# Three output projections go from plain float32 products to products of split operands in three passes, with their weights split in halves on ScalarE and GpSimd

## The chip, the core and the metric

The kernel runs on one core of a Trainium2 chip. The time is that of the device for one launch, in microseconds (us). Five engines work side by side, each with its own queue of instructions in program order: PE is TensorE (matrix products), DVE is VectorE, ACT is ScalarE, POOL is GpSimd, and SP issues the transfers. They wait for one another only by semaphores that the program names. On TensorE the profile shows weight loads (PEld) apart from the products (PE).

## The reference

Four layers of a transformer on 512 tokens of width 1024; the first two also carry 256 context tokens. All of it is float32. Each layer is an attention of some kind, an output projection and a residual sum; the last two layers have a gated feed-forward block behind that. The three output projections that the change touches are these products of a 512x1024 activation with a 1024x1024 weight:

```
y = jnp.dot(o.reshape(h.shape[0], h.shape[1], C_WIDTH) * jax.nn.silu(z_x), w_out)   # odd_mixer, od_w_out: "od_out"
...
x = x + gate * y
```

The third and fourth layer multiply their attention's result by even_w_out_2 ("e2_out") and odd_w_out_2 ("df_out") in the same way and add it to x without a gate.

## The kernel before, in words

Activations lie with features on the 128 partitions and tokens along the free dimension: X is 8 chunks of 128 features x 512 tokens. Weights come from HBM as a stream of tiles of 128x1024 float32 (512 KB), one for each 128 columns of output, into a ring of 8 slots (WT). SP refills a slot when the semaphore tile_used says that PE is through with the tile before it; w_ready{slot} tells that a tile has landed. STREAM sets the order of the tiles: od_out (8 tiles), e2_in (24), e2_out (8), up0 (44), down0 (22), df_in (24), df_out (8), up1 (44), down1 (22).

There are two ways to multiply. The three output projections use the plain one, project_pe (L277): for each of 8 tiles 8 products of 128x128 by 128x512 in float32, 64 in all, straight from the tile in WT and the attention's output (QO or OFE). Most other products use split operands: an activation or a weight x is written as hi, which is x rounded to the format fp32r (written by ACT), and lo = x - hi (written by DVE or POOL), and the product is hi*hi + hi*lo + lo*hi, three passes in fp32r. For that each weight tile has to be split before PE can use it.

- e2_in, df_in (class Projected, PE at L767 to L769), up0 and up1 (split_w_act, PE at L607 to L609) split whole tiles: ACT writes hi (1024 columns), DVE writes lo, into W_SPLIT with two places. Their first two tiles have a place of their own, W_EARLY, so that the first four tiles are split while the projection before still runs; PE takes tiles 0 and 1 interleaved (first_two_pe, L580 to L582), as chunks of the input become ready.
- ev_in, ev_out and the odd layer's input split in halves of 512 columns: ACT writes hi of a half (L513, L1360, L1369), POOL writes lo (L532, L1522, L1531), into W_HALF, which holds one half for h=0 and one for h=1. ACT may write half h of the next tile only when PE has used that half (half_used, tile_used). This is a ring: PE frees a half, ACT, then POOL refill it while PE works on the other.

Around an output projection the order is this. The attention's last unit ends with a DVE instruction (finish, L1781, or L1920 in the fourth layer) that raises at_out; PE waits for it (att.wait) and starts. For each finished tile t DVE adds it to X (residual_one, L652 with a gate, L650 without), ACT writes H_HI, chunk t of the next block's input times its gain (late_hi_act, L358), and DVE writes H_LO (residual_split_dve, L401). Before, DVE and ACT come to this only after they have split the next block's weight tiles 0 to 3, which arrive one by one as PE frees slots. Behind the last tile ACT squares X (L367) and DVE sums the squares (L377) for the norm.

Of the kernel before, what the change touches and what calls it, by code (L numbers as in the profile page):

```python
# [77 lines left out]
def program(nc, tokens, cond, weights, vec, con, gate_w, rpb, late, lam_in, out):  # L78
    ctx = ExitStack()
    with ctx:  # L80
# [79 lines left out]
        W_EARLY = over("W_EARLY", "SB", BIG + 4096, [128, 2, 2, TILE])  # L160

        def split_of(t):

            return W_EARLY[:, t] if t < 2 else W_SPLIT[:, t % 2]

# [185 lines left out]

        def late_hi_act(act, name):

            h0 = split_at[name][0]
            prev = LATE_NORMS[name][1]
            for c in range(KC):
                act.wait_ge(sem("evac_dve"), evacuated(prev)[1] + c + 1)
                act.activation(H_HI[:, c, :], X[:, c, 0:L], ACT.Identity, bias=NIL, scale=gain_late(name, c)).then_inc(sem("h_hi"), 1)  # L358
# [51 lines left out]
        def split_w_act(act, name, take, before=None):  # L410
# [3 lines left out]
            def body(q, s, rnd, slot):  # L414
                t = 8 * q + s if isinstance(q, int) else None
                if t == 0:
                    before(act)
                if t == 4:
                    late_hi_act(act, name)
                    late_squares_act(act, name)  # L420
                act.wait_ge(sem(f"w_ready{slot}"), (rnd + 1) * 16)
                if t is None or t >= 4:

                    act.wait_ge(sem("tile_used"), q * 8 + (g0 + s - 1))
                dst = W_SPLIT[:, s % 2] if t is None else split_of(t)
                act.activation(dst[:, 0, :], W[:, slot, :], ACT.Copy).then_inc(sem("w_hi"), 1)  # L426
# [34 lines left out]
        def low_w_dve(v, name, t, slot):  # L461

            w0 = split_at[name][1]
            v.wait_ge(sem("w_hi"), w0 + t + 1)
            v.tensor_tensor(split_of(t)[:, 1, :], W[:, slot, :], split_of(t)[:, 0, :].bitcast(F32), ALU.subtract)\
             .then_inc(sem("w_low"), 1)


        half_at = {"ev_in": 0, "ev_out": EV_CHUNKS, "od_q": EV_CHUNKS + 8}
# [96 lines left out]
        def first_two_pe(pe, name, banks_free):  # L566
# [3 lines left out]
            for k in range(KC + 1):  # L570
                for t in range(2):
# [7 lines left out]
                    hi, lo = (W_EARLY[:, t, x, c * 128:c * 128 + 128] for x in range(2))  # L579
# [142 lines left out]
        class Projected:  # L722
# [77 lines left out]
            def act(self, act, before=None):  # L800
                if before:
                    before(act)
                for t in range(26):
                    if t == (3 if self.early else 4):
# [3 lines left out]
                    if t < 24:  # L808
# [5 lines left out]
                        act.activation(split_of(t)[:, 0, :], W[:, (self.g0 + t) % SLOTS, :], ACT.Copy).then_inc(sem("w_hi"), 1)  # L814
# [7 lines left out]
                    if t < 4:  # L822
                        continue
                    if t == 4:
# [18 lines left out]
            def low(self, v, t):  # L843
                v.wait_ge(sem("w_hi"), self.w0 + t + 1)
                v.tensor_tensor(split_of(t)[:, 1, :], W[:, (self.g0 + t) % SLOTS, :], split_of(t)[:, 0, :].bitcast(F32), ALU.subtract)\  # L845
# [14 lines left out]
            def dve(self, v, add):  # L860
                for t in range(3 if self.early else 4):
                    self.low(v, t)
                residual_split_dve(v, self.name, add)
                if self.early:
                    self.low(v, 3)
# [20 lines left out]
            def values(self, eng):  # L886

                eng.wait_ge(sem("v_out"), self.value0 + 8)

# [283 lines left out]
        class Window:  # L1173
# [75 lines left out]
            def out_pe(self, pe):  # L1249
                for t in range(8):  # L1250
                    if t >= 4:
                        pe.wait_ge(sem("evac_dve"), self.d_ev + t - 3)
                    for h in range(2):
                        pe.wait_ge(sem("half_lo"), 2 * (self.gate0 + t) + h + 1)
                        for c in range(4 * h, 4 * h + 4):
                            if t == 0:
                                pe.wait_ge(sem("od_lo"), c + 1)
# [20 lines left out]
            def first_pe(self, pe):  # L1278
                pe.wait_ge(sem("first_lo"), 4)
                pe.wait_ge(sem("rs_log"), self.i + 1)  # L1280
                for c in range(KC):
                    pe.wait_ge(sem("od_lo"), KC + c + 1)
# [94 lines left out]
            def out_act(self, act):  # L1377
                for k, c in enumerate(self.order):
                    if c < 4:
                        act.wait_ge(sem("at_out"), att_mla.b["out"] + 2 * c + 2)  # L1380
                    act.activation(self.O_HI[:, k, :], PROJ[:, ZA + c, :], ACT.Copy).then_inc(sem("od_hi"), 1)
                for t in range(1, 8):
# [3 lines left out]
                    if t in (3, 4):  # L1386
                        act.wait_ge(sem(f"raw_in{t - 3}"), 32)
                        act.activation(self.FIRST[:, t - 3, 0, :], self.RAW[:, t - 3, :], ACT.Copy).then_inc(sem("od_hi"), 1)
# [7 lines left out]
                for c in range(KC):  # L1396
                    act.wait_ge(sem("od_normed"), KC + c + 1)
                    act.activation(HN_HI[:, c, 0:L], H[:, c, 0:L], ACT.Identity, bias=MOD[:, 24 + c, 0:1]).then_inc(sem("od_hi"), 1)
# [1407 lines left out]
```

## Time and profile before

| what | value |
|---|---|
| median of 3 runs | 2560.61 us (2560.12 to 2560.93) |
| the profiled execution: its time / its span | 2561.2 us / 2559.4 us |
| PE busy / DVE / ACT / POOL | 95% / 45% / 38% / 12% |
| mean granted TensorE clock | 0.983 |

The span runs from the first to the last instruction; 1.8 us of the execution's time lie outside it. All times in rows are us from the span's start. L numbers are lines of the kernel before. A row of the timeline gives start, duration, engine, line, operation, what it writes and reads and how many instructions are merged into it (xN); in square brackets the idle time before it and who ended it. Matrix products overlap: a product has a record of some 0.39 us, but the next one starts 0.23 us later, so the cost of one is the distance of starts. A plain float32 product shows as two records. In the clock's column 1.00 is the level of 2.4 GHz and 0.50 that of 1.2 GHz.

### The profile page before, as it was taken

The page shows a single profiled execution, that of the slowest core. Times are in us where ns is not written, and L with a number is a line of the kernel's source. Part 1 is how long each engine was busy: PE and PEld are TensorE (multiplying, and loading weights), DVE is VectorE, ACT ScalarE, POOL GpSimd, SP SyncE. Part 2 cuts the span into 40 slices and gives each one's busy share as a digit, 9 for nine tenths or more (in the row PEclk, how much of TensorE's full clock was granted, in tenths as well). Part 3 has the DMA queues.
Part 4 walks back from the last instruction along what each step waited for, and adds up shares of the span by engine and source line. Part 5 has one row for each costly group of instructions (what it writes and reads, how often), then busy time and mean ns, then how long its engine had stood idle before and what let it go on. Part 6 is the DMA issues. An engine that isn't in the chain of part 4 may idle for free.

```text
span 2559.4 us, 32847 instructions
## 1 busy us (share of the span) xinstructions
PE 2440.0 (95%) x12608; PEld 1799.0 (70%) x12608; DVE 1140.5 (45%) x1867; ACT 969.6 (38%) x1596; POOL 306.4 (12%) x206
## 2 busy tenths in 40 slices
PE   7999899889999999999999999999999889999998
PEld 4888665356878876664776568888877654888886
DVE  4000542544442204553345347666454462666744
ACT  4111434444344424552325343333252461433323
POOL 2233001100223330000000000003400000000142
PEclk9999799999999999999999999999999999999999
DMA  7112241010132222102220022323222101323231
GB/s 298 58 58 66 75 149 49 9 50 1 42 109 65 68 73 75 51 18 97 91 82 26 26 91 91 98 90 99 92 90 83 50 1 58 99 91 98 91 99 41
DMA packets 51872, 191.67 MB, mean 75 GB/s; under 512 B 5755, under 2 KB 6139, under 8 KB 51484
## 3 DMA queue, kind: packets, MB, share of 16 engines
q1 hardware_dynamic: 51740, 189.83, 22.5%
q8 instruction: 93, 1.52, 0.2%
q14 instruction: 39, 0.32, 0.0%
HBM read 187.71 MB, written 2.10 MB: 74 GB/s over the span
## 4 chain that ended last, share of the span: by engine, by line
PE 88%; ACT 4%; DVE 4%; issue 2%; DMA 0%; POOL 0%; SPq 0%; ACTq 0%; DVEq 0%; POOLq 0%
PE PS L277 7%; PE PS L609 6%; PE PS L607 6%; PE PS L608 6%; PE PS L1631 5%; PE PS L1658 4%; PE PS L2239 3%; PE PS L2241 3%; PE PS L2240 3%; PE PS L1644 3%; PE PS L1338 3%; PE PS L561 3%; PE PS L562 3%; PE PS L560 3%; PE PS L938 2%; PE PS L769 2%
## 5 line engine op out<-in xcount | busy, mean ns | idle before, releaser
L457 POOL TENSOR_TENSOR W_SPLIT<-WT,W_SPLIT 128x1024 fp32r<-128x1024 f32 x44 | 106.6, 2424 | 1455.4 <-ACT W_SPLIT L449 1331.9
L607 PE MATMUL PS<-H_HI,W_SPLIT 128*128 128x512 f32 x672 | 265.5, 395 | 0.0
L609 PE MATMUL PS<-H_HI,W_SPLIT 128*128 128x512 f32 x672 | 264.9, 394 | 0.0
L608 PE MATMUL PS<-H_LO,W_SPLIT 128*128 128x512 f32 x672 | 264.6, 394 | 0.0
L426 ACT ACTIVATE W_SPLIT<-WT 128x1024 fp32r<-128x1024 f32 x84 | 89.0, 1060 | 290.5 <-PE PS L609 267.3
L277 PE MATMUL PS<-SB,WT 128*128 128x512 f32 x384 | 167.3, 598 | 5.2 <-DVE SB L1781 3.1
L2570 DVE TENSOR_TENSOR W_SPLIT<-WT,W_SPLIT 128x1024 fp32r<-128x1024 f32 x80 | 98.0, 1225 | 151.8 <-ACT W_SPLIT L426 151.7
L2555 DVE TENSOR_TENSOR G_LO<-SB,G_HI 128x512 fp32r<-128x512 f32 x44 | 102.6, 2331 | 115.0 <-ACT G_HI L2395 115.0
L608 PEld LDWEIGHTS PS<-H_LO,W_SPLIT 128*128 128x128 f32 x672 | 126.0, 188 | 30.3 <-issue 0.5
L607 PEld LDWEIGHTS PS<-H_HI,W_SPLIT 128*128 128x128 f32 x672 | 126.2, 188 | 30.0 <-issue 0.5
L609 PEld LDWEIGHTS PS<-H_HI,W_SPLIT 128*128 128x128 f32 x672 | 126.2, 188 | 29.7
L277 PEld LDWEIGHTS PS<-SB,WT 128*128 128x128 f32 x384 | 73.3, 192 | 97.4 <-issue 91.5
L1644 PEld LDWEIGHTS PS<-SB 128*128 128x128 f32 x768 | 84.4, 142 | 79.6 <-issue 68.8
L2239 PE MATMUL PS<-G_HI,W_SPLIT 128*128 128x512 f32 x352 | 138.8, 394 | 0.2
L2241 PE MATMUL PS<-G_HI,W_SPLIT 128*128 128x512 f32 x352 | 138.0, 392 | 0.0
L2240 PE MATMUL PS<-G_LO,W_SPLIT 128*128 128x512 f32 x352 | 136.6, 388 | 0.0
L1644 PE MATMUL PS<-SB 128*128 128x128 f32 x768 | 112.9, 281 | 21.8 <-ACT SB L1705 19.2
L562 PE MATMUL PS<-HN_HI,W_HALF 128*128 128x512 f32 x368 | 124.1, 337 | 0.0
L561 PE MATMUL PS<-HN_LO,W_HALF 128*128 128x512 f32 x368 | 124.1, 337 | 0.0
L560 PE MATMUL PS<-HN_HI,W_HALF 128*128 128x512 f32 x368 | 123.7, 336 | 0.0
L845 DVE TENSOR_TENSOR W_SPLIT<-WT,W_SPLIT 128x1024 fp32r<-128x1024 f32 x44 | 53.9, 1226 | 154.6 <-ACT W_SPLIT L814 154.6
L1705 ACT ACTIVATE SB<-PS 128x512 f32<-128x512 f32 x120 | 64.8, 581 | 144.4 <-PE PS L1644 144.4
(322 smaller groups left out, 5158.5 us busy)
## 6 DMA issues: line engine op xcount, KB each, us to landing
WT<-weights SPq DMA_DIRECT2D x316, 512.0 KB, 3.5
SB<-weights SPq DMA_DIRECT2D x13, 512.0 KB, 12.7
SB<-rpb SPq DMA_DIRECT2D x8, 512.0 KB, 5.1
HT<-rpb SPq DMA_DIRECT2D x8, 512.0 KB, 4.4
XT<-tokens SPq DMA_DIRECT2D x4, 768.0 KB, 6.9
out<-HT SPq DMA_DIRECT2D x4, 512.0 KB, 2.6
SB<-late SPq DMA_DIRECT2D x1, 1280.0 KB, 5.7
SB<-con SPq DMA_DIRECT2D x1, 1248.0 KB
```

What stands on the lines that cost most here:

```text
L277: last = pe.matmul(PS[0:m, bank, 0:hi - lo], W[:, slot, c * 128:c * 128 + m], src[:, c, lo:hi], start=(c == 0), stop=(c == k - 1))
L560: pe.matmul(dst, hi, HN_HI[:, c, at:end], start=(c == 0), stop=False)
L561: pe.matmul(dst, hi, HN_LO[:, c, at:end], start=False, stop=False)
L562: last = pe.matmul(dst, lo, HN_HI[:, c, at:end], start=False, stop=(c == KC - 1))
L607: pe.matmul(PS[:, s, :], hi, H_HI[:, c, :], start=(c == 0), stop=False)
L608: pe.matmul(PS[:, s, :], hi, H_LO[:, c, :], start=False, stop=False)
L609: last = pe.matmul(PS[:, s, :], lo, H_HI[:, c, :], start=False, stop=(c == KC - 1))
L1631: last = pe.matmul(PS[:, self.bank(s, a) + b // 512, 0:e - b], self.q_of(pair, a)[:, 128 * t:128 * t + 128], self.k_of(pair, a)[:, lo + b: ...
L1644: last = pe.transpose(PS[:, 4 + k % 2, (b - b0) * 128:(b - b0) * 128 + 128], self.p(s, b // nb)[:, (b % nb) * 128:(b % nb) * 128 + 128], I ...
L2239: pe.matmul(PS[:, n, :], hi, G_HI[:, s % 2, :], start=first, stop=False)
L2240: pe.matmul(PS[:, n, :], hi, G_LO[:, s % 2, :], start=False, stop=False)
L2241: last = pe.matmul(PS[:, n, :], lo, G_HI[:, s % 2, :], start=False, stop=end)
```

## The change

The three projections get a class Output. PE multiplies with split operands, three passes per chunk. The attention's output O is split chunk by chunk: ACT writes O_HI (L934 of the changed kernel), DVE writes O_LO over O itself (L949). The weight tiles are split in halves of 512 columns, hi on ACT (L929) and lo on POOL (L965), into a new OUT_HALF with one place for each half; the first tile's halves are split ahead (before the attention od, and at tile 22 of e2_in and df_in). The work for the next block is woven in tile by tile: at tile t ACT writes the halves of tile t+1, then H_HI of chunk t, then hi of one whole tile of the next block (t = 1 to 4); DVE adds tile t, writes H_LO of chunk t-1 and lo of one whole tile (four times). up0 and up1 get an early place at another address, W_EARLY_UP.

```diff
+        class Output:
+            def pe(self, pe):
+                pe.wait_ge(sem("evac_dve"), ev_base[self.name][1])
+                for t in range(8):
+                    for h in range(2):
+                        pe.wait_ge(sem("half_lo"), 2 * (self.half0 + t) + h + 1)
+                        for c in range(4 * h, 4 * h + 4):
+                            if t == 0:
+                                pe.wait_ge(sem("o_lo"), self.lo0 + c + 1)
+                            hi, lo = (OUT_HALF[:, h, k, (c % 4) * 128:(c % 4) * 128 + 128] for k in range(2))
+                            pe.matmul(PS[:, t, :], hi, self.O_HI[:, c, :], start=(c == 0), stop=False)
+                            pe.matmul(PS[:, t, :], hi, self.O_LO[:, c, :], start=False, stop=False)
+                            last = pe.matmul(PS[:, t, :], lo, self.O_HI[:, c, :], start=False, stop=(c == KC - 1))
+                        last.then_inc(sem("tile_used" if h else "half_used"), 1)
+            def hi(self, act, t, h):
+                g = self.g0 + t
+                act.wait_ge(sem(f"w_ready{g % SLOTS}"), (g // SLOTS + 1) * 16)
+                if t and h == 0:
+                    act.wait_ge(sem("half_used"), self.used0 + t)
+                elif t:
+                    act.wait_ge(sem("tile_used"), g)
+                act.activation(OUT_HALF[:, h, 0, :], W[:, g % SLOTS, h * 512:h * 512 + 512], ACT.Copy).then_inc(sem("half_hi"), 1)
+            def act(self, act):
+                for c in range(KC):
+                    act.wait_ge(sem("at_out"), self.att.b["out"] + c + 1)
+                    act.activation(self.O_HI[:, c, :], self.O[:, c, :], ACT.Copy).then_inc(sem("o_hi"), 1)
+                f0 = FIRST_TILE[self.following]
+                for t in range(8):
+                    if t < 7:
+                        self.hi(act, t + 1, 0)
+                        self.hi(act, t + 1, 1)
+                    late_hi_one(act, self.following, t)
+                    if 1 <= t < 5:
+                        k = t - 1
+                        act.wait_ge(sem(f"w_ready{(f0 + k) % SLOTS}"), ((f0 + k) // SLOTS + 1) * 16)
+                        act.activation(split_of(self.following, k)[:, 0, :], W[:, (f0 + k) % SLOTS, :], ACT.Copy).then_inc(sem("w_hi"), 1)
+            def dve(self, v, add):
+                for c in range(KC):
+                    v.wait_ge(sem("o_hi"), self.hi0 + c + 1)
+                    v.tensor_tensor(self.O_LO[:, c, :], self.O[:, c, :], self.O_HI[:, c, :].bitcast(F32), ALU.subtract).then_inc(sem("o_lo"), 1)
+                h0 = split_at[self.following][0]
+                for c in range(KC + 1):
+                    if c < KC:
+                        add(c)
+                    if c >= 1:
+                        v.wait_ge(sem("h_hi"), h0 + c)
+                        v.scalar_tensor_tensor(H_LO[:, c - 1, :], X[:, c - 1, 0:L], gain_late(self.following, c - 1),
+                                               H_HI[:, c - 1, :].bitcast(F32), ALU.mult, ALU.subtract).then_inc(sem("h_lo"), 1)
+                    if 2 <= c < 6:
+                        low_w_dve(v, self.following, c - 2, (FIRST_TILE[self.following] + c - 2) % SLOTS)
+            def pool(self, g):
+                for t in range(8):
+                    for h in range(2):
+                        g.wait_ge(sem("half_hi"), 2 * (self.half0 + t) + h + 1)
+                        g.tensor_tensor(OUT_HALF[:, h, 1, :], W[:, (self.g0 + t) % SLOTS, h * 512:h * 512 + 512],
+                                        OUT_HALF[:, h, 0, :].bitcast(F32), ALU.subtract).then_inc(sem("half_lo"), 1)
...
-            project_pe(pe, "od_out", 8, QO, KC, L)
+            out_od.pe(pe)
...
-            project_pe(pe, "e2_out", 8, OFE, KC, L)
+            out_e2.pe(pe)
...
-            project_pe(pe, "df_out", 8, OFE, KC, L)
+            out_df.pe(pe)
```

What this does to DVE's queue at the first of the three projections (od_out), from the attention's last instruction on. In the kernel before (L1781 ends the attention, L845 are the next block's weight tiles, L652 the residual sums, L401 H_LO):

```order
L1781 TENSOR_TENSOR SB<-PS,SB 128x512
L845 TENSOR_TENSOR W_EARLY<-WT,W_EARLY 128x1024 x2
L845 TENSOR_TENSOR W_SPLIT<-WT,W_SPLIT 128x1024 x2
L652 SCALAR_TENSOR_TENSOR XT<-PS,SB,XT 128x512 x2
L401 SCALAR_TENSOR_TENSOR H_LO<-XT,SB,H_HI 128x512
```

In the changed kernel, at the same place of DVE's queue (L949 is O_LO, L655 the residual sums, L956 H_LO, L466 the next block's weight tiles):

```order
L1859 TENSOR_TENSOR SB<-PS,SB 128x512
L949 TENSOR_TENSOR O_LO_65<-SB,O_HI_64 128x512 x8
L655 SCALAR_TENSOR_TENSOR XT<-PS,SB,XT 128x512 x2
L956 SCALAR_TENSOR_TENSOR H_LO<-XT,SB,H_HI 128x512
L655 SCALAR_TENSOR_TENSOR XT<-PS,SB,XT 128x512
L956 SCALAR_TENSOR_TENSOR H_LO<-XT,SB,H_HI 128x512
L466 TENSOR_TENSOR W_EARLY<-WT,W_EARLY 128x1024
L655 SCALAR_TENSOR_TENSOR XT<-PS,SB,XT 128x512
L956 SCALAR_TENSOR_TENSOR H_LO<-XT,SB,H_HI 128x512
L466 TENSOR_TENSOR W_EARLY<-WT,W_EARLY 128x1024
```

So eight O_LO now stand between the attention's end and the residual sums, and each of the four weight tiles stands right behind an H_LO.

ACT's queue at the same place, before (L1705 belongs to the attention; L814 the weight tiles, L358 H_HI, L367 the squares):

```order
L1705 ACTIVATE SB<-PS 128x512 x2
L814 ACTIVATE W_EARLY<-WT 128x1024 x2
L814 ACTIVATE W_SPLIT<-WT 128x1024 x2
L358 ACTIVATE H_HI<-XT,SB 128x512 x8
L367 ACTIVATE XT<-XT 128x2x256 x8
```

and in the changed kernel (L934 O_HI, L929 hi of the halves of od_out's tiles, L359 H_HI, L944 the next block's tiles):

```order
L1783 ACTIVATE SB<-PS 128x512 x2
L934 ACTIVATE O_HI_64<-SB 128x512 x8
L929 ACTIVATE OUT_HALF<-WT 128x512 x2
L359 ACTIVATE H_HI<-XT,SB 128x512
L929 ACTIVATE OUT_HALF<-WT 128x512 x2
L359 ACTIVATE H_HI<-XT,SB 128x512
L944 ACTIVATE W_EARLY<-WT 128x1024
L929 ACTIVATE OUT_HALF<-WT 128x512 x2
L359 ACTIVATE H_HI<-XT,SB 128x512
L944 ACTIVATE W_EARLY<-WT 128x1024
```

Between two pairs of halves, on which PE now waits, ACT has an H_HI that waits for DVE's residual sum and, four times, a whole tile of the next block. POOL, which had nothing in these stretches, gets 16 lo halves in each.

## Rows read from the trace of the kernel before

**Rows 1.** The page: the chain that ended last, shares of the span by engine.
```profile
PE 88%; ACT 4%; DVE 4%; issue 2%; DMA 0%; POOL 0%; SPq 0%; ACTq 0%; DVEq 0%; POOLq 0%
```

**Rows 2.** Timeline of PE: the three output projections, and what follows the first.
```profile
1151.60 55.20 PE L277 MATMUL PS<-SB,WT 128*128 128x512 f32 x128 [1.52 <-DVE SB L1781]
1206.23 0.79 PE L580 MATMUL PS<-H_HI,W_EARLY 128*128 128x512 f32 x1
...
1442.88 55.20 PE L277 MATMUL PS<-SB,WT 128*128 128x512 f32 x128 [1.56 <-DVE SB L1781]
...
2117.52 56.90 PE L277 MATMUL PS<-SB,WT 128*128 128x512 f32 x128 [2.13 <-DVE SB L1920]
```

**Rows 3.** Timeline of PE: first product of e2_in's tile 2 and of tile 3.
```profile
1217.77 0.40 PE L767 MATMUL PS<-H_HI,W_SPLIT 128*128 128x512 f32 x1
...
1223.34 0.39 PE L767 MATMUL PS<-H_HI,W_SPLIT 128*128 128x512 f32 x1
```

**Rows 4.** Timelines of DVE and PE: two attentions' ends, and ev_out's start.
```profile
1150.85 0.69 DVE L1781 TENSOR_TENSOR SB<-PS,SB 128x512 f32<-128x512 f32 x1
...
651.69 0.42 DVE L1781 TENSOR_TENSOR SB<-PS,SB 128x256 f32<-128x256 f32 x1
...
653.25 0.47 PE L1261 MATMUL PS<-O_HI,W_HALF 128*128 128x512 f32 x1 [2.07 <-DVE O_LO L1462]
```

**Rows 5.** Windows behind three starts of PE (ev_out, df_out, od_out); the clock stands behind POOL.
```profile
654.20:657.60 3.40, 3.40 (x12) 2.92 (x12) 3.40 (x5) 1.02 (x2) 0.00 (x0) 0.50 0.00 0
2118.50:2122.00 3.50, 3.50 (x6) 1.44 (x5) 0.00 (x0) 0.00 (x0) 0.00 (x0) 0.51 0.00 0
1151.60:1155.00 3.40, 3.40 (x8) 1.62 (x9) 0.00 (x0) 0.00 (x0) 0.00 (x0) 1.00 0.73 211
```

**Rows 6.** Timelines of ACT, POOL and PE: the ring of halves, odd layer's input.
```profile
888.20 0.63 ACT L1369 ACTIVATE W_HALF<-WT 128x512 fp32r<-128x512 f32 x1 [2.15 <-PE PS L1310]
...
886.13 1.30 POOL L1531 TENSOR_TENSOR W_HALF<-WT,W_HALF 128x512 fp32r<-128x512 f32 x1 [1.48 <-ACT W_HALF L1369]
888.91 2.01 POOL L1531 TENSOR_TENSOR W_HALF<-WT,W_HALF 128x512 fp32r<-128x512 f32 x1 [1.48 <-ACT W_HALF L1369]
...
890.50 0.39 PE L1310 MATMUL PS<-HN_HI,W_HALF 128*128 128x512 f32 x1
...
891.32 0.39 PE L1309 MATMUL PS<-HN_LO,W_HALF 128*128 128x512 f32 x1
```

**Rows 7.** Timelines of DVE and POOL where both read two tensors from SBUF.
```profile
738.47 0.74 DVE L1482 SCALAR_TENSOR_TENSOR HN_LO<-HT,SB,HN_HI 128x512 fp32r<-128x512 f32 x1
739.13 0.68 DVE L1479 TENSOR_TENSOR HT<-HT,SB 128x512 f32<-128x512 f32 x1
...
738.65 2.34 POOL L1531 TENSOR_TENSOR W_HALF<-WT,W_HALF 128x512 fp32r<-128x512 f32 x1 [22.09 <-ACT W_HALF L1369]
...
876.33 2.98 DVE L1513 SCALAR_TENSOR_TENSOR SB<-SB 128x768 f32<-128x768 f32 x2
...
876.48 2.01 POOL L1531 TENSOR_TENSOR W_HALF<-WT,W_HALF 128x512 fp32r<-128x512 f32 x1 [1.48 <-ACT W_HALF L1369]
```

**Rows 8.** Timelines of ACT and DVE beside od_out: weight tiles, H_HI, residual sums.
```profile
1162.58 1.06 ACT L814 ACTIVATE W_EARLY<-WT 128x1024 fp32r<-128x1024 f32 x1 [16.43 <-DMA WT<-weights]
...
1188.30 0.82 ACT L358 ACTIVATE H_HI<-XT,SB 128x512 fp32r<-128x512 f32 x1 [0.78 <-DVE XT L652]
...
1163.74 1.23 DVE L845 TENSOR_TENSOR W_EARLY<-WT,W_EARLY 128x1024 fp32r<-128x1024 f32 x1 [12.19 <-ACT W_EARLY L814]
...
1199.97 0.75 DVE L652 SCALAR_TENSOR_TENSOR XT<-PS,SB,XT 128x512 f32<-128x512 f32 x1 [5.46 <-PE PS L277]
```

**Rows 9.** Timeline of ACT: idle time where first halves go; df attention's end.
```profile
982.39 1.28 ACT L1696 ACT_TABLE_LOAD   x1 [4.15 <-DVE SB L1747]
...
1345.68 1.06 ACT L814 ACTIVATE W_SPLIT<-WT 128x1024 fp32r<-128x1024 f32 x1 [4.49 <-PE PS L787]
...
2116.05 0.63 ACT L1888 ACTIVATE SB<-SB 128x512 f32<-128x512 f32 x1
```

More of the change, by code:

```diff
@@ L408, in behind, with split_w_act @@
             return (q if s >= k else q - 1), (s - k) % 8
-        def split_w_act(act, name, take, before=None):
+        def split_w_act(act, name, take):
             g0, (h0, w0, n) = FIRST_TILE[name], split_at[name]
@@ L415, in body @@
                 t = 8 * q + s if isinstance(q, int) else None
-                if t == 0:
-                    before(act)
+                if t is not None and t < 4:
+                    return
                 if t == 4:
-                    late_hi_act(act, name)
                     late_squares_act(act, name)
                 act.wait_ge(sem(f"w_ready{slot}"), (rnd + 1) * 16)
[L422 to L426, printed above, removed]
+                act.wait_ge(sem("tile_used"), q * 8 + (g0 + s - 1))
+                act.activation(W_SPLIT[:, s % 2, 0, :], W[:, slot, :], ACT.Copy).then_inc(sem("w_hi"), 1)
                 if t == 4:
@@ L464, in low_w_dve @@
             v.wait_ge(sem("w_hi"), w0 + t + 1)
-            v.tensor_tensor(split_of(t)[:, 1, :], W[:, slot, :], split_of(t)[:, 0, :].bitcast(F32), ALU.subtract)\
+            v.tensor_tensor(split_of(name, t)[:, 1, :], W[:, slot, :], split_of(name, t)[:, 0, :].bitcast(F32), ALU.subtract)\
              .then_inc(sem("w_low"), 1)
-        half_at = {"ev_in": 0, "ev_out": EV_CHUNKS, "od_q": EV_CHUNKS + 8}
+        half_at = {"ev_in": 0, "ev_out": EV_CHUNKS, "od_q": EV_CHUNKS + 8,
+                   "od_out": (EV_CHUNKS + 38, EV_CHUNKS + 40), "e2_out": (EV_CHUNKS + 46, EV_CHUNKS + 48),
+                   "df_out": (EV_CHUNKS + 54, EV_CHUNKS + 56)}
         def first_hi(act, t, h):
@@ L578, in first_two_pe @@
                         pe.wait_ge(sem("h_lo"), h0 + c + 1)
-                    hi, lo = (W_EARLY[:, t, x, c * 128:c * 128 + 128] for x in range(2))
+                    hi, lo = (early_of(name)[:, t, x, c * 128:c * 128 + 128] for x in range(2))
                     pe.matmul(PS[:, t, :], hi, H_HI[:, c, :], start=(c == 0), stop=False)
@@ L798, in pe, with act @@
                         pe.matmul(PS[:, 6 + r % 2, :], std[0], QKE[:, r, :], start=True, stop=True).then_inc(sem("qk_turned"), 1)
[L800 to L804, printed above, removed]
+            def act(self, act, output):
+                for t in range(0 if self.early else 4, 26):
+                    if t == 3:
                         late_hi_act(act, self.name)
@@ L823, in act @@
                         continue
+                    if t == 22:
+                        output.hi(act, 0, 0)
+                        output.hi(act, 0, 1)
                     if t == 4:
@@ L858, in turned, with dve @@
                 v.tensor_tensor(x, self.T1[:, r % 2, :], self.T2[:, r % 2, :], ALU.add).then_inc(sem("qk_done"), 1)
[L860 to L863, printed above, removed]
+            def dve(self, v, add=None):
                 if self.early:
+                    for t in range(3):
+                        self.low(v, t)
+                    residual_split_dve(v, self.name, add)
                     self.low(v, 3)
@@ L1380, in out_act @@
                         act.wait_ge(sem("at_out"), att_mla.b["out"] + 2 * c + 2)
-                    act.activation(self.O_HI[:, k, :], PROJ[:, ZA + c, :], ACT.Copy).then_inc(sem("od_hi"), 1)
+                    act.activation(self.O_HI[:, k, :], PROJ[:, ZA + c, :], ACT.Copy).then_inc(sem("o_hi"), 1)
                 for t in range(1, 8):
@@ L1985, in program @@
                              mask=causal_mask(lambda u: 0), values_in=qkv_df.values, sm_at=PE_AT + 5120, rt_at=PE_AT + 6144, sq_at=PE_AT + 6656, wide=512)
+        OUT_HALF = over("OUT_HALF", "HT", KC * L, [128, 2, 2, TILE // 2])
+        out_od = Output(0, "od_out", "e2_in", att_od, 8192)
+        out_e2 = Output(1, "e2_out", "up0", att_e, 4096)
+        out_df = Output(2, "df_out", "up1", att_df, 4096)
         G = view(BIG, FC, L)
@@ L2602, in down_one @@
                 return add
-            def low_first(name):
-                for t in range(4):
-                    low_w_dve(v, name, t, (FIRST_TILE[name] + t) % SLOTS)
-            qkv_e2.dve(v, residual_one(v, "od_out", L, lambda t, b: MOD[:, 40 + t, 0:1]))
+            out_od.dve(v, residual_one(v, "od_out", L, lambda t, b: MOD[:, 40 + t, 0:1]))
+            qkv_e2.dve(v)
             qkv_e2.heads(v)
```

66 lines of the change are left out of this document (42 added, 24 removed).

## The prediction

> **What bounds the kernel now.** I read the chain that ended last first: 88% of it is PE [rows 1], and DMA has no share, so time is won where PE does less or waits less. Then PE's timeline at the three output projections [rows 2]. Each runs without a gap from its first product to its last. The reader is to see two things: 64 float32 products take 1206.23 - 1151.60 = 54.63 us from the first to the next block's first product, 0.854 us each; and PE starts right behind the attention's last DVE instruction (1150.85 + 0.69 = 1151.54 [rows 4], PE at 1151.60), after a pause of 1.52, 1.56 and 2.13 us. The record of each projection is 0.57 us longer than that distance (1151.60 + 55.20 against 1206.23), so e2_out takes 54.63 and df_out 56.90 - 0.57 = 56.33 us. The three make **165.6 us**, all on the path. Beside them DVE and ACT are idle most of the time and POOL altogether.
>
> **The change part by part.**
>
> *The products.* The passes in fp32r are in the trace: e2_in's tile 2 begins at 1217.77, tile 3 at 1223.34 [rows 3], so 24 passes take 5.57 us, 0.232 each. Three passes per chunk are 0.696 us where the float32 product took 0.854. A projection of 192 passes takes 8 x 5.57 = 44.56 us.
>
> *The switch of format.* The first fp32r product behind float32 ones has a record of 0.79 us instead of 0.39 [rows 2, 3]. This switch now lies at the projection's beginning, where PE's start is counted anew below (and that row includes it). At the end it goes: -0.40 us.
>
> *The start.* PE may start when O_LO of chunk 0 is there, and DVE writes it only behind the attention's last instruction. ev_out already starts so: DVE ends at 651.69 + 0.42 = 652.11 and PE begins at 653.25, 1.14 us later [rows 4]. The pieces there are 768 wide. By the records of 512 and 1024 columns, 0.68 and 1.23 us [rows 7, 8], 256 columns less are 0.27 us less, so 0.87 us against 0.06 before: **+0.81 us**. The other seven chunks follow at some 0.6 us each and PE needs one each 0.70 us, so they hide behind its passes. ACT's O_HI is earlier still: in the last attention ACT is free at 2116.05 + 0.63 = 2116.68 [rows 9], and DVE's last instruction there ends some 0.8 us behind that, as PE's start at 2117.52 shows.
>
> *The clock.* A pause costs more than itself. Behind the pause of 2.07 us ahead of ev_out and that of 2.13 us ahead of df_out the granted clock falls to the 1.2 GHz level for 3.4 us; behind the pause of 1.52 us it stays at 2.4 GHz [rows 2, 4, 5]. At half the clock 3.4 us of work are 1.7 us of delay, and df_out's 56.33 - 54.63 = 1.70 us show just that. With 0.81 us more the pauses become 2.33, 2.37 and 2.94 us, all on the longer side. I therefore charge **1.7 us** to each projection (df_out has it already). Bounds: 0 and 1.7.
>
> *The ring of halves.* This is the part that could go wrong: POOL is much slower than DVE at it, and the two halves give each refill only the 12 passes, 2.79 us, of the other half. The odd layer's input runs the same ring at that very pitch: POOL starts at 886.13 and 888.91, 2.78 us apart [rows 6]. ACT takes the half 0.71 us ahead of POOL, POOL needs 1.30 us, and PE does not wait. When POOL took 2.01 us, 0.71 more, PE's two steps from 890.50 to 891.32 took 0.82 us instead of 0.46: a wait of 0.36. So the ring has **0.35 us to spare** per half.
>
> *POOL against DVE.* Why 2.01 us? In the like case DVE's instruction with two inputs from SBUF begins at 876.33, POOL's split at 876.48 has to wait, and then the second such DVE instruction waits for POOL (the two last 2.98 us together, where one of 512 columns takes 0.74) [rows 7]. The one shuts the other out. The last 0.12 us of a DVE record don't count: POOL's record of 2.34 us from 738.65 has its own 1.30 us from 739.69, and DVE's ran to 739.13 + 0.68 = 739.81. Now lay out a tile from its first pass. The tile before ends at +0.16; ACT starts hi of half 1 at +0.25, POOL wants to start at +0.96. DVE starts the residual sum at about +0.2, and 0.66 us later (the distance 738.47 to 739.13 [rows 7]) H_LO, from +0.86. It lets go of SBUF 0.62 us on, at +1.48. POOL is 0.52 us late, and 0.17 of it is more than the ring spares. This happens in the six tiles in which an H_LO follows a residual sum: **+1.0 us** per projection. Then DVE's weight tile waits until POOL ends at +2.8 and holds SBUF until +3.9; POOL's next split is wanted at 2.79 + 0.96 = +3.75: 0.15 late, which is spared. Bounds for the whole item: 0, and the second rival below.
>
> *ACT's queue.* Behind hi of half 1 ACT waits for the residual sum (done at about +0.98), writes H_HI (0.82) and the weight tile (1.06) [rows 8] and is free at +2.86; the next half is wanted at 2.79 + 0.25 = +3.04. It fits, with 0.18 us left. The tile of the next block lands 4.1 us behind the end of the projection's tile whose slot it takes (1162.58 against 1151.60 + 6.83 [rows 2, 8]); ACT asks for it one tile and 1.8 us later, 7.4 us. Nothing waits.
>
> *What moves at no cost.* The first tile's halves take ACT 2 x 0.63 us [rows 6] inside idle stretches of 4.15 and, ahead of tile 23 of e2_in, 4.49 us [rows 9]; POOL is idle there. Without that cover it would be 1.3 us each. The next block's four whole-tile splits and H_HI, H_LO were beside PE's work before and still are.
>
> **The sum.** Per projection 44.56 + 0.81 + 1.7 + 1.0 - 0.40 = 47.67 us, three of them 143.0 us against 165.6: a gain of 22.6 us. The profiled execution took 2561.2 us, 0.6 us over the median. 2561.2 - 22.6 = 2538.6, in terms of the median **2538.0 us**.
>
> **A rule on the shared pair.** The Trainium skill (SBUF — State Buffer, "SBUF: two separate sides") says that a VectorE instruction with two SBUF inputs and a GpSimd instruction exclude each other by a lock held for the whole instruction, not by sharing bandwidth. The rows of 2.01 us agree. Taken to the letter, with H_LO's whole record of 0.74 us instead of 0.62, POOL would be 0.12 us later in 18 tiles, 2.2 us in all: 2540.2 us. I take the 0.62, as worked out from 738.65 above.
>
> **The rivals.**
> 1. *Forecast: POOL gets its turn behind H_LO.* 2538.0 us. Without the drop of the clock at od_out and e2_out 2534.6, at none of the three 2532.9; with the whole-record lock 2540.2. For it: both DVE instructions of L1513 stood back to back, and POOL still went between them [rows 7]. Chance 0.68, own range 2531 to 2542.
> 2. *DVE keeps the lock through H_LO and the weight tile behind it.* At 738.47 and 739.13 DVE's two instructions went first and POOL's record grew to 2.34 us [rows 7]. Against it: that second instruction had no semaphore to wait for in the program, while L1513's and all of the new ones have one. If it holds, POOL is held until 1.48 + 0.05 + 1.11 = +2.64, 1.68 us late, a PE wait of 1.33 instead of 0.17, in four tiles of each projection: 12 x 1.16 = 13.9 us more, **2551.9 us**. Chance 0.20.
> 3. *Both, and more delays in the ring.* If every one of the 42 refills lost half a microsecond beyond what the ring spares, 21 us would go and 2559 us be left, no change that can be told. Rows of 1.30 us speak against it wherever DVE is quiet, and DVE has only some 2.5 us of work in each 5.57. Chance 0.08 for this and all between 2552 and 2566.
> 4. *Slower: the next block's weight tile in ACT's queue.* It stands between two refills, so a late transfer stops PE through ACT and POOL, where before it stopped nothing. It has 7.4 - 4.1 = 3.3 us in hand, and 0.5 more from ACT and the ring. To pay back 22.6 us with 12 such waits takes 1.9 us each, a landing 9.8 us behind the slot's release; from 2.3 us each on the kernel is slower by over 0.2%, about **2566 us**. All transfers seen here land in half that. Chance 0.04.
>
> **How the numbers follow.** A measurement of this kernel can tell about 0.2%, 5.1 us, from no change. Faster by more than that is all below 2555.5 us: 0.68 + 0.20 and a part of the third, 0.91. Within 0.2%: 0.05. Slower: 0.04. The range reaches over the forecast's own bounds and the second rival, **2531 to 2553 us**.
>
> **What would show it.** In the changed profile PE's starts of tiles should lie 5.57 to 5.75 us apart and the first pass 0.87 us behind the attention's last DVE instruction; POOL's 48 splits should last 1.30 us, or 1.8 in six per projection, and 2.9 to 3.0 us in four if the second rival holds. The clock should be 0.50 in a stretch of 3.4 us behind each start. From there to the next block's first product 47.7 us, or 52.3 with the second rival. The forecast is wrong if ACT's waits for a transfer end behind PE's need, if POOL's record in the new ring is above 2 us in most tiles, or if PE gains a pause ahead of the next block's first tile, where H_LO of the last chunks comes as late after the last product as before.

## The result

| | before | after |
|---|---|---|
| median | 2560.36 us (2555.07 to 2560.93, 4 runs) | 2528.39 us (2527.76 to 2538.56, 4 runs) |
| the profiled execution: time / span | 2561.2 / 2559.4 us | 2528.24 / 2526.5 us |

The ratio is 0.9889, with a 95% interval of 0.9861 to 0.9917: faster. It is the ratio of the means, 2559.2 and 2530.8 us, which lie 28.4 us apart; the medians lie 32.0 us apart, as one of four runs in each row stands far from the rest. The forecast was 2538.0 us, a ratio of 0.9912. That is inside the interval, but the median lies 2.6 us below the range of 2531 to 2553. A repeat (below) gave 2530.97 us and 0.9892.

The page of the changed kernel: span, busy time of each engine, and the chain that ended last (compare [rows 1]).

```profile
span 2526.5 us, 33417 instructions
PE 2404.6 (95%) x12800; PEld 1828.9 (72%) x12800; DVE 1166.3 (46%) x1891; ACT 1011.4 (40%) x1668; POOL 376.9 (15%) x254
...
PE 88%; ACT 5%; DVE 5%; issue 2%; DMA 1%; SPq 0%; POOL 0%; DVEq 0%; ACTq 0%; POOLq 0%
```

POOL has 70 us more work and is still not on the chain. PE has 35 us less.

Windows of the changed kernel: the three projections from the first product to the next block's first, then the four stretches around them. The columns are window, its length, PE, PEld, DVE, ACT, POOL busy with their instructions, granted clock, share of DMA, GB/s.

```profile
1145.61:1192.74 47.13, 47.13 (x193) 36.80 (x193) 22.22 (x24) 18.26 (x25) 20.81 (x14) 0.96 0.37 120
1428.22:1473.46 45.24, 45.23 (x192) 35.71 (x193) 21.82 (x24) 20.95 (x30) 20.84 (x14) 1.00 0.25 82
2093.26:2141.29 48.03, 48.03 (x192) 37.78 (x193) 21.80 (x24) 20.88 (x30) 20.73 (x14) 0.94 0.24 77
0.00:1145.61 1145.61, 1067.75 (x6616) 784.40 (x6617) 404.73 (x753) 460.15 (x764) 201.50 (x164) 0.98 0.21 73
1192.74:1428.22 235.48, 226.78 (x1355) 166.20 (x1354) 116.13 (x258) 98.40 (x219) 3.07 (x2) 1.00 0.17 57
1473.46:2093.26 619.80, 595.76 (x2654) 467.46 (x2652) 353.77 (x569) 255.22 (x428) 56.52 (x24) 0.99 0.24 78
2141.29:2526.50 385.21, 373.96 (x1603) 300.59 (x1601) 225.85 (x242) 137.50 (x174) 53.45 (x22) 0.99 0.26 86
```

By [rows 2] the three stretches took 54.63, 54.63 and 56.33 us before. They now take 140.4 us instead of 165.6, 25.2 less. The other 7.7 us of the span's difference of 32.9 lie outside, most of it ahead of od_out: 1145.61 against 1151.60, though the pause ahead of PE's start has grown by 0.8 us. Little in that stretch was changed, and the experiments ask first what this is.

The timeline of PE in the changed kernel: the first product of each of od_out's tiles, and of e2_in.

```profile
1145.61 0.47 PE L917 MATMUL PS<-O_HI,OUT_HALF 128*128 128x512 f32 x1 [2.33 <-DVE O_LO L949]
...
1152.84 0.39 PE L917 MATMUL PS<-O_HI,OUT_HALF 128*128 128x512 f32 x1
...
1158.44 0.39 PE L917 MATMUL PS<-O_HI,OUT_HALF 128*128 128x512 f32 x1
...
1164.16 0.39 PE L917 MATMUL PS<-O_HI,OUT_HALF 128*128 128x512 f32 x1
...
1169.88 0.39 PE L917 MATMUL PS<-O_HI,OUT_HALF 128*128 128x512 f32 x1
...
1192.74 0.39 PE L583 MATMUL PS<-H_HI,W_EARLY 128*128 128x512 f32 x1
```

The first tile takes 7.23 us (a drop of the clock), the second 5.60, the third and later ones 5.72. The first product of e2_in now has a record of 0.39 us and the next starts 0.23 later. Before, the record was 0.79 [rows 2].

The drops behind the starts of od_out and df_out, and the starts of two passes inside the second:

```profile
1147.10:1150.50 3.40, 3.40 (x10) 2.64 (x9) 2.58 (x5) 0.56 (x1) 0.00 (x0) 0.50 0.96 391
2093.30:2099.40 6.10, 6.10 (x15) 4.75 (x16) 4.02 (x7) 3.04 (x6) 0.00 (x0) 0.50 0.00 0
...
2094.25 0.63 PE L919 MATMUL PS<-O_HI,OUT_HALF 128*128 128x512 f32 x1
2094.68 0.63 PE L917 MATMUL PS<-O_HI,OUT_HALF 128*128 128x512 f32 x1
```

At 1.2 GHz a pass starts 0.43 us behind the one before, at 2.4 GHz 0.23 us. So a pass loses some 0.45 of its time at the low clock, not half: a drop of 3.4 us costs 1.55 us here, where it cost the plain float32 products 1.70 us (56.33 against 54.63).

DVE, POOL and ACT of the changed kernel in the fourth tile, which begins at 1164.16.

```profile
1164.36 0.75 DVE L655 SCALAR_TENSOR_TENSOR XT<-PS,SB,XT 128x512 f32<-128x512 f32 x1 [4.31 <-PE PS L919]
1165.02 0.74 DVE L956 SCALAR_TENSOR_TENSOR H_LO<-XT,SB,H_HI 128x512 fp32r<-128x512 f32 x1
1165.68 2.31 DVE L466 TENSOR_TENSOR W_EARLY<-WT,W_EARLY 128x1024 fp32r<-128x1024 f32 x1
...
1162.21 1.29 POOL L965 TENSOR_TENSOR OUT_HALF<-WT,OUT_HALF 128x512 fp32r<-128x512 f32 x1 [1.01 <-ACT OUT_HALF L929]
1165.12 1.79 POOL L965 TENSOR_TENSOR OUT_HALF<-WT,OUT_HALF 128x512 fp32r<-128x512 f32 x1 [1.63 <-ACT OUT_HALF L929]
1167.93 1.30 POOL L965 TENSOR_TENSOR OUT_HALF<-WT,OUT_HALF 128x512 fp32r<-128x512 f32 x1 [1.01 <-ACT OUT_HALF L929]
...
1165.86 1.04 ACT L944 ACTIVATE W_EARLY<-WT 128x1024 fp32r<-128x1024 f32 x1
1167.22 0.63 ACT L929 ACTIVATE OUT_HALF<-WT 128x512 fp32r<-128x512 f32 x1 [0.31 <-PE PS L919]
```

POOL's record starts 0.10 us after H_LO's and lasts 1.79 us instead of 1.29, and then DVE's weight tile lasts 2.31 us instead of 1.23: POOL had its turn between DVE's two instructions. The next split is undisturbed, at 1.30. ACT has 0.31 us in hand before its next half.

### The profile page after: what moved, and what is told of

Read it like the earlier page. It is cut to its first block, busy times and chain, and to the rows that moved or that the text cites. A ratio compares the mean times of both kernels' runs of the same rounds, so it can differ in the third digit from the quotient of the medians.

```text
span 2526.5 us, 33417 instructions
## 1 busy us (share of the span) xinstructions
PE 2404.6 (95%) x12800; PEld 1828.9 (72%) x12800; DVE 1166.3 (46%) x1891; ACT 1011.4 (40%) x1668; POOL 376.9 (15%) x254
## 3 DMA queue, kind: packets, MB, share of 16 engines
q8 instruction: 95, 1.56, 0.3%
## 4 chain that ended last, share of the span: by engine, by line
PE 88%; ACT 5%; DVE 5%; issue 2%; DMA 1%; SPq 0%; POOL 0%; DVEq 0%; ACTq 0%; POOLq 0%
PE PS L612 6%; PE PS L610 6%; PE PS L611 6%; PE PS L1709 5%; PE PS L1736 4%; PE PS L2328 3%; PE PS L2326 3%; PE PS L2327 3%; PE PS L1722 3%; PE PS L1416 3%; PE PS L564 3%; PE PS L565 3%; PE PS L563 3%; PE PS L1016 2%; PE PS L772 2%; PE PS L770 2%
## 5 line engine op out<-in xcount | busy, mean ns | idle before, releaser
L427 ACT ACTIVATE W_SPLIT<-WT 128x1024 fp32r<-128x1024 f32 x80 | 84.8, 1060 | 267.3 <-PE PS L612 267.3
L965 POOL TENSOR_TENSOR OUT_HALF<-WT,OUT_HALF 128x512 fp32r<-128x512 f32 x48 | 71.0, 1482 | 737.6 <-ACT OUT_HALF L929 737.6
L815 ACT ACTIVATE W_SPLIT<-WT 128x1024 fp32r<-128x1024 f32 x42 | 44.5, 1059 | 172.7 <-PE PS L772 114.6
```

## Experiments

**What is the gain outside the projections?** The kernel before and the changed kernel, each once more without an edit.

> The kernel before, unchanged, with a profile of its own, to see what the two first profiles differ by ahead of the change's place. In them the first float32 product of od_out starts at 1151.60 us before and the first split one at 1145.61 us after, and the time at the 1.2 GHz level up to there is 54.6 against 37.5 us. If this is the clock's own variation (A), this run's od_out starts anywhere between about 1145 and 1155 us, about half a microsecond earlier for each microsecond less at the low level, and the three stretches keep 54.63 us, or 56.3 with a drop of the clock in them. If it comes from something the change does (B), od_out starts at 1151.6 within 0.5 us again, with 54 to 55 us at the low level.

Measured: 2559.08 us (2555.47 to 2561.71, 10 runs), ratio 1.0001 (0.9991 to 1.0011). Windows of its profiled execution, up to od_out and od_out:

```profile
0.00:1148.52 1148.52, 1070.84 (x6616) 784.88 (x6616) 404.62 (x751) 454.86 (x754) 200.35 (x162) 0.98 0.21 73
1148.52:1203.16 54.64, 54.64 (x129) 24.27 (x129) 13.76 (x17) 9.81 (x11) 0.00 (x0) 1.00 0.31 103
```

The very same program reaches od_out 3.1 us earlier than in [rows 2], while the stretch itself repeats to 0.01 us. That is case A. This run's pauses were 1.52, 1.56 and 2.13 us again.

> The changed kernel, unchanged, with more runs beside the kernel before. If the forecast's sum is right and the rest of the first difference was the clock's variation outside the three stretches (A), the median lies near 2533 us, some 25 us under that of the kernel before beside it, and the runs of both spread over 5 to 10 us. If the change gives 32 us of its own (B), it is 2528 us or less while the kernel before is at 2558 to 2560 us.

Measured: 2530.97 us (2527.86 to 2537.86, 5 runs) against 2561.02 (2554.99 to 2562.17, 9 runs), ratio 0.9892 (0.9875 to 0.991). Its pauses (2.34, 2.38, 2.95 us) and stretches (47.14, 45.24, 48.01) repeat the first execution's to 0.03 us; od_out starts at 1150.47, 4.9 us later. The median lies between the two that were expected (2533 and 2528). So the pieces that the change touches are the same each time, and what varies is the clock elsewhere. To take it out, I added up for every profiled execution (two passes aside, which has less work) PE's busy time in the stretches where its granted clock is 0.50, and took half of it off the span, as for a float32 product, which takes twice as long there:

| kernel | span, us | PE busy at 1.2 GHz, us | span less half of it |
|---|---|---|---|
| before | 2559.4 | 75.0 | 2521.9 |
| before, again | 2555.0 | 65.2 | 2522.4 |
| after | 2526.5 | 60.8 | 2496.1 |
| after, again | 2531.2 | 71.2 | 2495.6 |
| wait moved ahead | 2531.3 | 66.5 | 2498.0 |
| H_LO earlier | 2527.2 | 67.1 | 2493.6 |
| early start | 2521.8 | 67.8 | 2487.9 |
| both | 2521.3 | 72.6 | 2485.0 |
| all O_LO first | 2546.5 | 77.5 | 2507.7 |

Executions of one kernel, whose spans differ by 4.4 and 4.7 us, agree to 0.5 us in the last column. In it the change is worth 25.8 to 26.8 us. With the passes' 0.45 (0.455 by their starts) in place of the half, the two executions of before come to 2525.3 us both, those of after to 2498.8 us both, 26.5 us apart. The stretches give the same without this correction. Without drops the three took 163.9 us before (3 x 54.63) and take 136.1 us now (od_out 45.60 us in the execution of the next experiment, which had no drop there; e2_out 45.24; df_out, whose tiles behind the first take what e2_out's do, counted as e2_out). That is 27.8 us, less 2.45 us of longer pauses, plus 1.2 us for the switch of format: 26.6 us.

**Does DVE keep SBUF through two instructions?** The second rival rested on a second instruction that has no wait. Here DVE's wait for the weight tile's hi stands ahead of H_LO, so the weight tile follows H_LO with no wait between.

```diff
                     if c >= 1:
+                        if 2 <= c < 6:
+                            v.wait_ge(sem("w_hi"), split_at[self.following][1] + c - 1)
                         v.wait_ge(sem("h_hi"), h0 + c)
...
-                        low_w_dve(v, self.following, c - 2, (FIRST_TILE[self.following] + c - 2) % SLOTS)
+                        low_w_now(v, self.following, c - 2, (FIRST_TILE[self.following] + c - 2) % SLOTS)
```

> The changed kernel with one wait moved: DVE waits for the next block's weight tile (hi) ahead of H_LO and not between H_LO and the weight tile's lo, so that these two stand back to back with no wait between them, four times in each projection. If DVE keeps the shared pair when its next instruction has no wait (A, as at 738.47 and 739.13 us in the kernel before), POOL's split grows from 1.80 to about 2.95 us in 12 places, the tile distance there from 5.72 to about 6.9 us, and the time by 12 to 14 us. If POOL gets its turn in any case, since it has asked first (B), the records stay at 1.8 us and the time within 2 us.

Measured: 2533.68 us (2532.51 to 2535.3, 4 runs), ratio 0.9903 (0.9887 to 0.992). DVE and POOL in its fourth tile of od_out:

```profile
1167.74 0.74 DVE L963 SCALAR_TENSOR_TENSOR H_LO<-XT,SB,H_HI 128x512 fp32r<-128x512 f32 x1
1168.40 2.33 DVE L471 TENSOR_TENSOR W_EARLY<-WT,W_EARLY 128x1024 fp32r<-128x1024 f32 x1
...
1167.84 1.80 POOL L972 TENSOR_TENSOR OUT_HALF<-WT,OUT_HALF 128x512 fp32r<-128x512 f32 x1 [1.64 <-ACT OUT_HALF L934]
```

Nothing has moved in the ring: POOL still goes between, no record of the ring is above 1.82 us, the tiles are 5.72 and 5.66 us apart. The rival is refuted here, whether the second instruction waits or not. The time is 5.3 and 2.7 us above the medians of the changed kernel's two sets of runs, where within 2 us was expected, and 1.9 to 2.4 us above it in the table's last column. In the profiled execution this lies behind df_out, where the edit changes nothing. Windows of od_out (no drop here) and of the stretch behind df_out:

```profile
1149.88:1195.48 45.60, 45.60 (x193) 35.71 (x193) 22.24 (x24) 18.26 (x25) 20.91 (x14) 1.00 0.36 125
...
2143.76:2531.33 387.57, 376.34 (x1603) 301.16 (x1601) 226.09 (x242) 137.51 (x174) 53.59 (x22) 0.99 0.26 86
```

The stretch behind df_out took 385.21 us in after (above). In the second half of it 100 passes take 23.33 us instead of 22.89; the execution with two passes (below) has this too. Its cause stays open.

Why POOL's record from 738.65 [rows 7] was 2.34 us, with both of DVE's ahead of it, stays open.

**What does the pause at the start cost?** Chunks 0 to 3 of O are split before DVE's last instruction of the attention, and PE starts tile 0 on them; it waits for the attention's end only at tile 1. The diff shows od_out; the other two are changed in the same way.

```diff
                 for t in range(8):
+                    if t == 1:
+                        self.att.wait(pe)
...
             def act(self, act):
-                for c in range(KC):
-                    act.wait_ge(sem("at_out"), self.att.b["out"] + c + 1)
-                    act.activation(self.O_HI[:, c, :], self.O[:, c, :], ACT.Copy).then_inc(sem("o_hi"), 1)
+                self.o_hi(act, range(4, KC))
...
-            att_od.wait(pe)
             out_od.pe(pe)
...
-            att_od.act(act)
+            att_od.act(act, lambda: out_od.o_hi(act, range(4)))
             out_od.act(act)
...
-            att_od.dve(v)
+            att_od.dve(v, lambda: out_od.o_lo(v, range(4)))
```

> The changed kernel with the first four chunks of O split before the attention's last DVE instruction, and PE free to begin tile 0 without waiting for that instruction (it waits for the whole attention ahead of tile 1). The pauses of 2.33, 2.38 and 2.95 us ahead of the three projections should go to under 0.3 us, 7 us in all. If a drop of the clock follows a pause of 2 us or more (A), the drops behind the starts of od_out and df_out go too, 1.7 to 3 us each, and the time falls by 10 to 12 us. If the drops come whatever the pause (B), they stay and the gain is 7 us or less.

Measured: 2523.38 us (2520.74 to 2527.76, 4 runs), ratio 0.9864 (0.9847 to 0.988). PE's timeline at od_out, and the windows of the three stretches:

```profile
1146.75 0.28 PE L1755 MATMUL PS<-SB 128*64 128x128 f32 x2
1146.96 0.50 PE L919 MATMUL PS<-O_HI,OUT_HALF 128*128 128x512 f32 x1
...
1146.96:1192.58 45.62, 45.62 (x195) 35.74 (x193) 22.04 (x23) 18.91 (x26) 20.87 (x14) 1.00 0.38 124
1427.18:1472.45 45.27, 45.27 (x194) 35.73 (x193) 21.95 (x24) 21.15 (x31) 20.95 (x14) 1.00 0.25 82
2090.82:2136.62 45.80, 45.65 (x195) 35.52 (x194) 22.22 (x25) 21.83 (x32) 21.22 (x14) 1.00 0.24 80
```

The pauses are gone and so are the drops behind them. In the last column of the table this is worth 7.7 to 8.2 us, the three pauses' 7.7. The 10 to 12 us that were expected with the drops gone (A) did not come: PE worked 67.8 us at 1.2 GHz in this execution, between after's 60.8 and 71.2. So no saving from the missing drops shows in the total.

**What does POOL's delay cost?** H_LO of chunk t follows the residual sum of chunk t at once, and waits for ACT's H_HI, instead of following the next residual sum.

```diff
-                for c in range(KC + 1):
-                    if c < KC:
-                        add(c)
-                    if c >= 1:
-                        v.wait_ge(sem("h_hi"), h0 + c)
...
+                for c in range(KC):
+                    add(c)
+                    v.wait_ge(sem("h_hi"), h0 + c + 1)
...
-                    if 2 <= c < 6:
+                    if 1 <= c < 5:
```

> The changed kernel with H_LO of chunk t right behind the residual sum of tile t (where it must wait for ACT's H_HI) and not that of chunk t-1. H_LO then asks for SBUF at about +1.75 us, while POOL holds it from +0.96 to +2.26. If the tile's 5.66 to 5.72 us are 5.57 plus what POOL comes late behind H_LO (A), POOL's records are 1.30 us throughout (or up to 0.2 more for the half that follows the weight tile), the tiles 5.57 to 5.61 us apart and the time 2 to 2.5 us less. If the distance comes from the ring's own length of refill (B), it stays at 5.66 to 5.72 us and the time within 0.5 us.

Measured: 2530.65 us (2523.18 to 2533.23, 4 runs), ratio 0.9886 (0.9865 to 0.9906), which can't be told from after. DVE and POOL in its fourth tile:

```profile
1163.65 0.75 DVE L655 SCALAR_TENSOR_TENSOR XT<-PS,SB,XT 128x512 f32<-128x512 f32 x1 [1.79 <-PE PS L919]
1165.29 0.98 DVE L954 SCALAR_TENSOR_TENSOR H_LO<-XT,SB,H_HI 128x512 fp32r<-128x512 f32 x1 [0.89 <-ACT H_HI L359]
...
1164.42 1.30 POOL L963 TENSOR_TENSOR OUT_HALF<-WT,OUT_HALF 128x512 fp32r<-128x512 f32 x1 [1.41 <-ACT OUT_HALF L929]
```

Now POOL is first and DVE waits for it (0.98 us instead of 0.74). POOL keeps its 1.30 us here; its other records behind the first tile are 1.28 to 1.39 us, one 1.60. Every tile behind the first is 5.60 or 5.61 us long, as in case A.

Both edits together:

> The early start of e3 and the order of e4 together. If both act by what they were made for (A), the pauses are gone, the tiles lie 5.60 us apart, the three stretches take 44.9 us each and the time is 2521 us, 2 to 2.5 us under e3. If e4's order only moves the wait elsewhere (B), it is that of e3.

Measured: 2523.78 us (2522.88 to 2524.67, 4 runs), ratio 0.9862 (0.9847 to 0.9878). Windows of the three stretches:

```profile
1150.59:1195.48 44.89, 44.89 (x194) 36.10 (x193) 20.91 (x24) 18.90 (x26) 18.79 (x14) 1.00 0.37 126
1430.16:1475.05 44.89, 44.89 (x194) 36.03 (x193) 20.84 (x25) 21.15 (x31) 18.45 (x14) 1.00 0.25 82
2090.66:2136.09 45.43, 45.29 (x196) 36.02 (x194) 21.12 (x26) 21.83 (x32) 18.78 (x14) 1.00 0.24 81
```

Against the early start alone the stretches are 0.73, 0.38 and 0.37 us shorter. That is the price of POOL's delay, 1.5 us in the three, measured with no drop of the clock in any. The table's last column has 2.9 us between the two; the rest lies ahead of od_out, where the two kernels do not differ. The medians don't show the gain at all (2523.78 against 2523.38, where 2521 was expected): they vary more than that. Both this version and the early start beat the kernel before and the changed one: none of their eight runs is above 2527.76 us, the fastest of the changed kernel's nine.

**How much does the ring spare?** One of the three passes (hi with O_LO) is left out, so that PE needs less time for a half than its refill does. The product then lacks that part.

```diff
                             pe.matmul(PS[:, t, :], hi, self.O_HI[:, c, :], start=(c == 0), stop=False)
-                            pe.matmul(PS[:, t, :], hi, self.O_LO[:, c, :], start=False, stop=False)
```

> The changed kernel without one of the three passes, hi of the weight times lo of the activation, in the three projections; its output lacks that product. PE's work of a tile falls from 5.57 to 3.71 us and a half's from 2.79 to 1.86 us. If the ring refills a half in 2.44 us (A: 2.79 less the 0.35 us to spare), a tile without a collision takes 4.88 us, and one in which POOL waits for H_LO up to 5.4 us, with PE waiting at each half. If the ring were much faster than that (B), a tile takes 3.75 us and each projection 30 us.

Measured: 2507.19 us in one run. PE's timeline, first products of od_out's tiles 1, 2 and 3, and of tiles 5 and 6:

```profile
1154.71 0.50 PE L917 MATMUL PS<-O_HI,OUT_HALF 128*128 128x512 f32 x1 [0.40 <-POOL OUT_HALF L964]
...
1159.00 0.50 PE L917 MATMUL PS<-O_HI,OUT_HALF 128*128 128x512 f32 x1 [0.28 <-POOL OUT_HALF L964]
...
1163.34 0.44 PE L917 MATMUL PS<-O_HI,OUT_HALF 128*128 128x512 f32 x1
...
1173.15 0.50 PE L917 MATMUL PS<-O_HI,OUT_HALF 128*128 128x512 f32 x1
...
1177.93 0.50 PE L917 MATMUL PS<-O_HI,OUT_HALF 128*128 128x512 f32 x1
```

A tile takes 4.29 us where POOL is undisturbed (1154.71 to 1159.00), though its 16 passes need 16 x 0.233 = 3.73. Neither expected figure (4.88 or 3.75) came. Where I had reckoned with two refills to a tile, the refill of one half runs beside PE's work on the other: a half's cycle is PE's 8 passes on it (1.87) and its refill, so the refill takes about 4.29 - 1.87 = 2.42 us. With three passes it has 2.80 us (12 x 0.233) for that: 0.38 to spare. Where POOL waits for H_LO a tile takes 4.78 us, 0.49 more: now the whole delay reaches PE.

**Does a longer pause add time at the low clock?** PE waits for all eight O_LO before its first pass.

```diff
                             if t == 0:
-                                pe.wait_ge(sem("o_lo"), self.lo0 + c + 1)
+                                pe.wait_ge(sem("o_lo"), self.lo0 + KC)
```

> The changed kernel with PE waiting for all eight chunks of O_LO before its first pass, so that the pauses ahead of the three projections grow by 7 x 0.61 = 4.3 us each, to 6.6, 6.7 and 7.2 us. If a long pause brings the drop of the clock (A), all three starts have one of 3.4 us or more, and the time is 12.9 + 1 to 5 us above that of the changed kernel, 2547 to 2552 us. If the drops are by chance (B), one or two of the three starts have none, as at 2.33 us.

Measured: 2548.31 us (2547.23 to 2548.32, 4 runs), ratio 0.9956 (0.9941 to 0.9971). PE's first products of the three:

```profile
1153.11 0.76 PE L917 MATMUL PS<-O_HI,OUT_HALF 128*128 128x512 f32 x1 [6.55 <-DVE O_LO L949]
...
1442.38 0.77 PE L917 MATMUL PS<-O_HI,OUT_HALF 128*128 128x512 f32 x1 [6.59 <-DVE O_LO L949]
...
2114.83 0.77 PE L917 MATMUL PS<-O_HI,OUT_HALF 128*128 128x512 f32 x1 [7.17 <-DVE O_LO L949]
```

Each pause is 4.2 us longer, 12.6 in all; in the table's last column the kernel is 11.6 to 12.1 us longer. The time is inside the 2547 to 2552 us of case A. All three starts have a drop; it begins inside the pause and lasts into the passes for 5.4, 2.8 and 2.9 us. The mean granted clock of the four runs is 0.979 to 0.981 where after has 0.981 to 0.986. Here the pauses do bring more time at 1.2 GHz, 77.5 us of PE's work.

## Why the prediction was right, and where its sum was off

| term, for the three together | forecast | measured |
|---|---|---|
| passes | 133.7 us | 134.4 (24 tiles x 5.60) |
| later start | +2.43 | +2.45 (2.33, 2.38, 2.95 against 1.52, 1.56, 2.13) |
| POOL's delay in the ring | +3.0 | +1.5 (early start against both) |
| switch of format | -1.2 | -1.2 (0.23 us instead of 0.64 to the next pass, each time) |
| clock, beyond before | +3.4 | no rise in the totals |

- **Bound and products.** PE sets the end, and a pass starts 0.233 us behind the one before: 5.60 us for a tile. I had 5.57 from e2_in [rows 3]. The three starts' drops aside, this 0.7 us too little and the 1.5 us too much at POOL partly cancel.
- **Start.** 0.81 us later each time, as worked out from 256 columns less: at od_out DVE's last instruction ends at 1144.74 and PE starts at 1145.61, 0.87 us behind it. The seven other chunks hid, and ACT's queue fitted with 0.31 us in hand in the fourth tile (forecast 0.18). No weight tile came late: the fourth rival, like the third, found nothing.
- **POOL against DVE.** The mechanism was right: POOL's record grew to 1.79 us at od_out and 1.74 at the others, forecast 1.8 in six splits per projection (od_out has five, and one of 1.51), and DVE's weight tile then waited for POOL. The delay of 0.50 or 0.45 us costs PE 0.12 or 0.06 us a tile, not 0.17: the delay is a little shorter than the forecast 0.52, and the ring spares 0.38, not 0.35. What is left of such a small difference is half of the forecast. In the row of 1165.12 POOL's own 1.29 us begin at 1165.62, 0.14 us before H_LO's record ends at 1165.76. The Trainium skill (SBUF — State Buffer, "SBUF: two separate sides") has the lock held for the whole instruction. For who excludes whom the trace agrees; by the record's end POOL's record would be 1.93 us, and here the measurement decides, as the prediction took it.
- **The clock is the step that failed.** "I therefore charge 1.7 us to each projection": a pause of 2.33 to 2.38 us was followed by a drop at 3 of 10 starts (after, its repeat, wait moved ahead, H_LO earlier, two passes), one of 2.95 at 5 of 5, one of 2.13 at 2 of 2 (before), one of 1.5 at none of 4, none without a pause at 6 starts. So a drop behind 2.33 us is not certain, and the forecast of a stretch of 3.4 us behind each start failed at e2_out. The place may count as much as the length: the pauses of 2.13 and 2.95 us are all ahead of df_out, which had a drop each time, and the prediction went by the length alone. Nor was the price right: 3.4 us cost the passes 1.55 us. In the profiled execution two of three starts had a drop, df_out's lasting 6.1 us, and they cost 4.3 us in all (7.23 - 5.67 and 8.46 - 5.67 us in the first tiles, where 5.67 us is such a tile without a drop), forecast 5.1. That it comes so near is luck: one drop too few, one nearly twice as long. Above all, the charge does not show as a rise of the total. PE worked 75.0 and 65.2 us at 1.2 GHz in the two executions of before, and 60.8 and 71.2 in those of after. The mean granted clock of the nine runs of after is 0.984, as is that of 22 runs of before; by an estimate, 3.4 us more of delay is some 7 us more at 1.2 GHz and would have lowered that mean by 0.0014, about twice the uncertainty of nine runs' mean (0.0006 by their spread). Whether the drops at the starts come in exchange for others isn't shown. Without the clock's term the forecast gain is 22.6 + 3.4 = 26.0 us, and 25.8 to 26.8 were measured: the other terms add up rightly.
- **The range.** Its low end, 2531, allowed for a case without drops (2532.9) and 1.9 us more, but not for the clock's own variation: before itself ran from 2552.24 to 2562.17 us. With it the range should have reached some 5 us lower.

What stays open: what decides whether a drop follows a pause of 2.3 us, and why the drops at the starts don't show in the total. Only places and lengths of the drops were seen, no cause.

## What to carry to other kernels

Here a float32 product of 0.854 us gave way to three passes of 0.70 us together; what decides whether that comes through is the ring behind it: compare the refill (ACT, POOL, their semaphores) with PE's time on the other half, and put DVE's two-input instructions where POOL is not due. A delay in that ring costs only what exceeds the slack. Where PE waits for an operand that is made piece by piece, let it start on the pieces that are ready: here that was worth 7.7 us, the tuning of the ring 1.5. And before explaining a difference of a few microseconds between two executions, take out PE's time at the low clock; here that turned 32.9 us in one pair of executions and 23.8 us in another into 25.8 and 26.8.

## What the runs showed of the hardware

- The time of one program varies by 10 us (before: 2552.24 to 2562.17), for the most part with the granted clock: 2552.24 us had a mean of 0.988, the runs near 2561 had 0.983 or 0.984. One run of 2558.3 us at 0.987 falls out of line.
- At 1.2 GHz the starts of passes lie 0.43 us apart against 0.23 at 2.4 GHz, so a drop costs less than half of its length.
- With DVE's instructions back to back, POOL got its turn between them at all 36 weight tiles of three executions (after, its repeat, wait moved ahead), and a DVE instruction that waits for POOL shows its wait inside its record (2.31 us instead of 1.23; 0.98 instead of 0.74), with no idle time beside it. A long record can be a wait.
- df_out's first tile is 6.15 us long even with the early start and no drop, 0.45 us more than at the others: PE waits there for the fifth chunk's O_LO. No run tried to win it.
